# Contiguous token layout, merged sample blocks, and an f32 attention-value product in two column groups

## The reference, cut to what matters

```python
m = silu(c) @ w_ada + b_ada                    # shift, scale and gate, twice
h = layer_norm(x) * (1 + scale1) + shift1
u, q, k, v = split(h @ w_in)                   # 512 columns each
pool = multiscale_pool(u) @ w_pool * pool_scale
z = q @ k.T * 64 ** -0.5                       # strictly causal
a = sigmoid(z)[t, s] * prod_{s < j < t} (1 - sigmoid(z)[t, j])
x = LN1(alpha * x + gate1 * (concat(pool, a @ v) @ w_o))
h = layer_norm(x) * (1 + scale2) + shift2
x = LN2(alpha * x + gate2 * ((silu(h @ w_g) * (h @ w_u)) @ w_down))
```

## Time and profile before

| | |
|---|---|
| median of 3 runs | 2767.44 us (2766.02 to 2767.84) |
| profiled execution, its own time | 2765.61 us |
| its span, first to last instruction | 2763.4 us |
| mean granted TensorE clock | 0.984 of full |
| PE busy | 2622.0 us (95%) |
| DVE busy | 1624.7 us (59%) |
| ACT busy | 1136.4 us (41%) |
| POOL busy | 645.0 us (23%) |

### The profile page before, as it was taken

One profiled execution on the slowest core, in us unless ns is written; L12 is line 12 of the kernel. 1 busy time (PEld: TensorE's weight loads), 2 busy tenths in 40 slices (PEclk: granted clock), 3 DMA queues, 4 the chain that ended last, 5 costly groups with the idle time before them and its releaser, 6 DMA issues.

```text
span 2763.4 us, 39203 instructions
## 1 busy us (share of the span) xinstructions
PE 2622.0 (95%) x15824; PEld 1430.6 (52%) x15824; DVE 1624.7 (59%) x2084; ACT 1136.4 (41%) x1616; POOL 645.0 (23%) x865
## 2 busy tenths in 40 slices
PE   6899899899898888999999999999999999999998
PEld 3444455344344333454566664456666544999733
DVE  4647654799999999889433233544323344644455
ACT  1522232778887888224322223222222322333331
POOL 1300000466666765223211110001111000111100
PEclk9899999999999999999999999999999999999999
DMA  6225678232323110322222224522322345433462
GB/s 233 94 67 201 234 259 237 74 92 73 81 77 85 24 60 13 129 92 86 71 77 84 62 77 130 198 92 77 100 62 74 106 139 166 119 98 88 127 202 104
DMA packets 262542, 308.25 MB, mean 112 GB/s; under 512 B 27694, under 2 KB 221038, under 8 KB 256603
## 3 DMA queue, kind: packets, MB, share of 16 engines
q1 hardware_dynamic: 243354, 236.54, 27.8%
q10 hardware_dynamic: 19008, 69.21, 7.6%
HBM read 267.32 MB, written 38.40 MB: 111 GB/s over the span
## 4 chain that ended last, share of the span: by engine, by line
PE 73%; DVE 14%; issue 5%; ACT 3%; POOL 1%; DMA 1%; SPq 0%; POOLq 0%; DVEq 0%; ACTq 0%
PE ps L2055 34%; PE ps L2089 18%; PE ps L1767 10%; DVE work L1413 3%; PE ps L2006 3%; DVE work L1429 3%; PE ps L1856 2%; PE ps L1880 2%; PE ps L1858 1%; ACT ps L976 1%; DVE work L1410 1%; DVE work L1582 1%; PE ps L1895 1%; DMA pool_dram<-work 1%; DVE work L1288 1%
## 5 line engine op out<-in xcount | busy, mean ns | idle before, releaser
L2055 PE MATMUL ps<-hidden_t,work 128*128 128x384 f16 (+2 forms) x7392 | 946.2, 290 | 0.6 <-DVE work L1632 0.6
L2055 PEld LDWEIGHTS ps<-hidden_t,work 128*128 128x128 f16 x7392 | 646.9, 98 | 298.7 <-issue 2.4
L2089 PE MATMUL ps<-work 128*128 128x512 f16 (+1 forms) x2244 | 489.3, 379 | 0.0
L1767 PE MATMUL ps<-hidden_t,work 128*128 128x512 f16 (+1 forms) x1920 | 355.7, 343 | 12.4 <-DVE hidden_t L1180 7.7
L2089 PEld LDWEIGHTS ps<-work 128*128 128x128 f16 (+1 forms) x2244 | 215.7, 98 | 272.7 <-issue 18.0
L740 POOL TENSOR_TENSOR work<-work 128x512 f32<-128x512 f32 (+2 forms) x320 | 304.9, 955 | 200.4 <-DVE work L1413 128.7
L787 POOL TENSOR_TENSOR work<-work 128x384 f16<-128x384 f32 (+1 forms) x154 | 118.0, 766 | 934.5 <-ACT work L1076 934.5
L1629 DVE SCALAR_TENSOR_TENSOR work<-ps,col,work 128x384 f32<-128x384 f32 (+1 forms) x154 | 80.9, 525 | 431.4 <-ACT work L1074 431.3
L1638 DVE SCALAR_TENSOR_TENSOR work<-work,col 128x1024 f16<-128x1024 f32 x132 | 168.1, 1280 | 227.2 <-ACT work L1086 227.2
L1086 ACT ACTIVATE work<-work,col 128x1024 f16<-128x1024 f32 x132 | 150.8, 1147 | 290.6 <-PE ps L2089 268.9
L1074 ACT ACTIVATE work<-ps,col 128x384 f32<-128x384 f32 (+1 forms) x154 | 77.7, 505 | 450.6 <-PE ps L2055 450.6
(11 more groups left out here) (209 smaller groups left out, 2442.9 us busy)
## 6 DMA issues: line engine op xcount, KB each, us to landing
work<-in_w_gu SPq DMA_DIRECT2D x132, 512.0 KB, 5.0
work<-in_w_down ACTq DMA_DIRECT2D x132, 512.0 KB, 3.6
work<-in_w_ada SPq DMA_DIRECT2D x24, 1024.0 KB, 5.3
work<-in_w_gu SPq DMA_DIRECT2D x22, 1024.0 KB, 5.4
work<-in_w_down SPq DMA_DIRECT2D x11, 1024.0 KB, 5.5
work<-in_x_prompt SPq DMA_DIRECT2D x8, 1024.0 KB, 7.0
work<-in_w_in SPq DMA_DIRECT2D x16, 512.0 KB, 6.7
out<-work SPq DMA_DIRECT2D x32, 256.0 KB, 5.6
```

The costliest lines, as they stand in the source:

```text
L1767: mm = pe.matmul(bank(blk, n, blk), B_HL[s][:, wh * KD * P + k * P:wh * KD * P + (k + 1) * P], moving(k, xh, blk), start=(k == 0 and (wh, ...
L2055: mm = pe.matmul(out, E_GHL[s][:, wh, k, w, :], x, start=(k == 0 and (wh, xh) == (0, 0)), stop=(k == KD - 1 and (wh, xh) == TERMS[-1]))
L2089: mm = pe.matmul(ps[0:rows, 2 * slot + half, :], E_HID[:, j, xh, at:at + rows], E_DHL[slab_home(g)][:, wh, 512 * half:512 * (half + 1)], s ...
```

## The change

What it does:

- `hidden_t` becomes [partition, k, part, 2080 tokens], the sample's 32 tokens right behind the prompt's 2048. `project` takes five blocks of 416 columns instead of 4 x 512 + 32, and the last gate/up group two blocks of 272 instead of 256, 256 and 32. `token_rows` waits for the block in which its 512 tokens end. `evac_pool` copies the last 32 columns of its last block separately.
- The attention weights stay f32: one copy of each turned tile, by ACT for three of four tiles and by DVE for every fourth (k % 4 == 1), scaled by `C_SMIX`. `weigh` multiplies them by the raw f32 values (64 columns), even key tiles into rows 0 to 63 of the bank and odd ones into rows 64 to 127, and PE's loop issues two `weigh` together every second step. On the diagonal a product with zeros opens rows 64 to 127. The value splits go. SP loads the next values after the queries and keys, once all weighing of the head before is done.
- Products with few stationary columns are spread over the four groups of 32 columns: the `w_ada` products at the start and in the attention, the mixing output of the sample, and the down products of the sample tile. The four parts are added by a product with `fold` (four stacked identities, [128, 32]); for the conditioning rows by an f32 product with `SEL`, its first two columns, in place of the transpose. Before `fold` is applied ACT (mixing) or DVE (down) copies 128 x 1024 out of PSUM.
- The sample tile moves behind tile 12 in the order of `down`'s fifth pass.

The diff, cut to its core:

```diff
-        hidden_t = sb("hidden_t", [P, NT + 1, KD, 2, P], f16)
+        cond_t = sb("cond_t", [P, KD, TS], f32)
+        fold = sb("fold", [P, TS], f32)
+        hidden_t = sb("hidden_t", [P, KD, 2, TOK], f16)
...
+        PB = TOK // 5
+        def copied(k):
+            by_dve = (k + 3) // 4
+            return (at_dve, by_dve) if k % 4 == 1 else (at_act, k + 1 - by_dve)
...
-        E_BLKS = [((0, 3), (3, 3)), ((6, 3), (9, 3)), ((12, 2), (14, 2), (NT, 1))]
+        E_BLKS = [((0, 384), (384, 384)), ((768, 384), (1152, 384)), ((1536, 272), (1808, 272))]
-        LN2_TILES = [*range(12), NT, *range(12, NT)]
+        LN2_TILES = [*range(13), NT, *range(13, NT)]
-                  ((9, 1), (10, 2), (11, 3)), ((12, 3), (13, 0)), ((14, 1), (15, 2), (16, 3))]
+                  ((9, 1), (10, 2), (11, 3)), ((12, 2), (13, 3)), ((14, 0), (15, 1), (16, 2))]
...
-                    sp.wait_ge(v_lo, h)
-                    load_v((h + 1) // 2, (h + 1) % 2)
                     sp.wait_ge(z_mm, 4 * NU * h)
                     load_qk((h + 1) // 2, (h + 1) % 2)
+                    sp.wait_ge(av_mm, 4 * NU * h)
+                    load_v((h + 1) // 2, (h + 1) % 2)
...
-            def at_high(k):
+            def at_copy(k):
                 act.wait_ge(at_mm, k + 1)
                 if k >= 4:
                     act.wait_ge(av_mm, k - 3)
-                act.activation(C_AT[k % 4][:, 0, j0:BLK], ps[:, 4 + k % 2, j0:BLK], ACT.Identity,
-                               scale=2.0 ** TOP).then_inc(at_act, 1)
+                act.activation(C_AT[k % 4][:, j0:BLK], ps[:, 4 + k % 2, j0:BLK], ACT.Identity,
+                               scale=c1(C_SMIX)).then_inc(at_act, 1)
...
-                if 5 <= m < NTILE + 5:
-                    at_high(m - 5)
+                if 5 <= m < NTILE + 5 and m % 4 != 2:
+                    at_copy(m - 5)
...
             for t in range(15):
+                if t == 14:
+                    act.wait_ge(so_mm, 2)
+                    act.activation(E_TMP, ps[:, 6:8, :].rearrange("p a n -> p (a n)"), ACT.Identity).then_inc(parts_copied, 1)
...
-            def at_low(k):
-                v.wait_ge(at_act, k + 1)
-                v.scalar_tensor_tensor(C_AT[k % 4][:, 1, j0:BLK], ps[:, 4 + k % 2, j0:BLK], 2.0 ** TOP,
-                                       C_AT[k % 4][:, 0, j0:BLK], ALU.mult, ALU.subtract).then_inc(at_dve, 1)
+            def at_copy(k):
+                v.wait_ge(at_mm, k + 1)
+                v.tensor_scalar(C_AT[k % 4][:, j0:BLK], ps[:, 4 + k % 2, j0:BLK], c1(C_SMIX), None,
+                                ALU.mult).then_inc(at_dve, 1)
...
-                    mm = pe.matmul(ps[0:2, s % 2, 0:256], CT[:, :, k], A_WADA[:, s, k, :],
-                                   start=(k == 0), stop=(k == KD - 1))
+                    at = TS * (k % 4)
+                    mm = pe.matmul(ps[at:at + TS, 2 + s % 2, 256:512], CT[:, k, :], A_WADA[:, s, k, :],
+                                   start=(k < 4), stop=(k >= 4))
...
             def weigh(k):
-                pe.wait_ge(at_dve, k + 1)
-                pe.matmul(ps[:, 6 + b % 2, j0:BLK], C_VHL[:, e, 4 * kc + kt, :], C_AT[k % 4][:, 0, j0:BLK],
-                          start=(kc == b and kt == 0), stop=(kc == 0 and kt == 3), skip_group_check=True)
-                pe.matmul(ps[0:HD, 6 + b % 2, j0:BLK], C_VHL[:, e, 4 * kc + kt, 0:HD], C_AT[k % 4][:, 1, j0:BLK],
-                          start=False, stop=(kc == 0 and kt == 3), skip_group_check=True).then_inc(av_mm, 1)
+                e, r = h % 2, HD * (kt % 2)
+                pe.wait_ge(*copied(k))
+                if kc == b and kt == 1:
+                    pe.matmul(ps[HD:P, 6 + b % 2, 0:P], C_TRI[:, 0:HD], ident_b[:, :], start=True, stop=False,
+                              skip_group_check=True)
+                pe.matmul(ps[r:r + HD, 6 + b % 2, j0:BLK], C_V[e][:, 4 * kc + kt, :], C_AT[k % 4][:, j0:BLK],
+                          start=(kc == b and kt < 2), stop=(kc == 0 and kt >= 2),
+                          skip_group_check=True).then_inc(av_mm, 1)
...
-                if m >= 7:
+                if m >= 8 and m % 2 == 0:
+                    weigh(m - 8)
                     weigh(m - 7)
...
+            def mix_out_sample():
+                for n in range(2):
+                    for i in range(3 * KD):
+                        k, (xh, wh) = i // 3, TERMS[i % 3]
+                        at = TS * (i % 4)
+                        mm = pe.matmul(ps[at:at + TS, 6 + n, :], hidden_t[:, k, xh, SEQ:TOK],
+                                       D_WO[k][:, wh, 512 * n:512 * (n + 1)], start=(i < 4), stop=(i >= 3 * KD - 4))
+            def fold_sample(bank0, done):
+                for n in range(2):
+                    mm = pe.matmul(ps[0:TS, bank0 + n, :], fold[:, :], E_TMP[:, 512 * n:512 * (n + 1)],
+                                   start=True, stop=True)
...
+                            if tile == NT:
+                                r, ends = TS * ((m + half) % 4), 4
+                    if p == 5 and (j, i) == (1, 2):
+                        pe.wait_ge(parts_copied, 2)
+                        fold_sample(6, parts_sum)
```

More of the change, by code:

```diff
@@ L284, in leave, with tile_cols @@
                 self.reg = None
[L286 to L295, removed]
+        PB = TOK // 5
+        def tile_cols(t):
+            return slice(t * P, t * P + P) if t < NT else slice(SEQ, TOK)
         TERMS = [(0, 0), (0, 1), (1, 0)]
@@ L747, in head_split @@
                 r = slice(HD * (h % 2), HD * (h % 2) + HD)
-                st = C_ST[b % 2][r, :].rearrange("p (i t) -> p i t", t=P)
-                dst = [hidden_t[r, 4 * b:4 * b + 4, 4 + h // 2, half, :] for half in range(2)]
+                st = C_ST[b % 2][r, :]
+                dst = [hidden_t[r, 4 + h // 2, half, BLK * b:BLK * (b + 1)] for half in range(2)]
                 pool.wait_ge(o_scaled, blk + 1)
@@ L905, in _ @@
                     act.wait_ge(q_stored[u], 32)
-                evac(c, u, B_QT[u])
+                for blk in range(5):
+                    evac(c, u, B_QT[u], blk)
                 high_part(c, B_QT[u])
             wpool_evac(3)
-            def evac_rows(c, s, blk):
-                act.wait_ge(proj_mm, 5 * c + blk + 1)
-                at, n = (BLK * blk, BLK) if blk < 4 else (SEQ, TS)
-                act.activation(B_VT[s][:, at:at + n], ps[:, blk, 0:n], ACT.Identity,
-                               scale=c1(C_W + 2 * s + 1)).then_inc(proj_out, 1)
             def rows_out(m):
@@ L1695, in _ @@
                         for n in first:
-                            summed(n)
+                            if LN2_TILES[n] == NT:
+                                parts_out(n)
+                            else:
+                                summed(n)
                     if 3 <= j < 3 + 2 * len(first):
                         (counted, normed)[(j - 3) % 2](first[(j - 3) // 2])
+                    if grp == 2 and j == 4:
+                        summed(first[1])
                 if grp < 2:
@@ L1739, in _ @@
             for q in range(16):
-                mm = pe.transpose(ps[:, 2, 2 * q:2 * q + 2], A_MROW[0:2, q * P:(q + 1) * P], ident[0:2, 0:2])
+                mm = pe.matmul(ps[:, 2, 2 * q:2 * q + 2], A_MROW[:, q * P:(q + 1) * P], SEL, start=True, stop=True)
             mm.then_inc(mod_turned, 1)
@@ L2087, in down @@
                     for half in range(2):
-                        for wh, xh in TERMS:
-                            mm = pe.matmul(ps[0:rows, 2 * slot + half, :], E_HID[:, j, xh, at:at + rows],
+                        for term, (wh, xh) in enumerate(TERMS):
+                            m = 3 * j + term
+                            if tile == NT:
+                                r, ends = TS * ((m + half) % 4), 4
+                            else:
+                                r, ends = 0, 1
+                            mm = pe.matmul(ps[r:r + rows, 2 * slot + half, :], E_HID[:, j, xh, at:at + rows],
                                            E_DHL[slab_home(g)][:, wh, 512 * half:512 * (half + 1)],
-                                           start=(j == 0 and (wh, xh) == (0, 0)),
-                                           stop=(j == NF - 1 and (wh, xh) == TERMS[-1]))
+                                           start=(m < ends), stop=(m >= 3 * NF - ends))
                     mm.then_inc(dn_mm, 1)
+                    if p == 5 and (j, i) == (1, 2):
+                        pe.wait_ge(parts_copied, 2)
+                        fold_sample(6, parts_sum)
             for grp in range(3):
```

228 lines of the change are left out of this document (108 added, 120 removed).

## The result

The changed kernel takes 2652.4 us, median of 4 runs (2648.2 to 2656.6), against 2766.7 us (2765.4 to 2767.8) for the kernel before on the same chip: a ratio of 0.9587, interval 0.957 to 0.9604. The profiled execution has a span of 2654.9 us, 108.5 under the span before.

| stage | before, us | after, us | difference | forecast |
|---|---|---|---|---|
| start, to the first projection | 77.6 | 74.0 | -3.6 | +4 |
| projections, to the first weighing | 431.3 | 430.2 | -1.1 | -3.5 |
| attention | 597.1 | 508.7 | -88.4 | -52 |
| mixing output | 205.2 | 208.5 | +3.3 | 0 |
| gate/up and down | 1452.2 | 1433.5 | -18.7 | -24 |

A forecast was written before the change was run, and what follows sets the result against it. VectorE was taken to bound the attention, and PE's streaming rate everything from 1311 us on. The sum was 2765.6 - 52 - 13 - 3.5 - 11 + 4 = 2690 us, 2692 on the median, range 2662 to 2762.

The forecast's parts named there:

- if B1 streams beside A2: Attention weighing: odd tile's first f32 instruction overlaps even tile's second, 1.52 us a pair (1.96 serial); 52 us gained.
- the pieces: Attention's 16 conditioning pieces, f32 products with w_ada: from 3.6 us each to nine slots, 2.0 us, plus 0.3 for turning.
- The pace: Attention time per head: PE's load of 60.8 us plus 12% for waits gives 68 us, from 74.6.
- Neither bounds any longer: Attention: with DVE down to about 414 us and ACT to about 437, neither sets the time.
- Latency: Attention rival: groups overlap, but the chain scan, scores, two sigmoids, scan sets 72 us a head; 2725 us, chance 0.10.
- absorbed case: Attention rival: no group overlap, PE's loss shrinks to 5%, 74.9 us a head, attention unchanged; 2757 us, chance 0.11.
- slower rival: Attention rival: no group overlap, f32 pair 1.96 us or more, 12% loss stays, 79.9 us a head; 2799 us, chance 0.12.
- The rule on weight loads: Attention, counter-argument: loads overlap products only across row groups, so a pair grows by four loads; given little weight.
- Gate/up: Last gate/up group: 32-column instructions go, 29.8 us, and 272-column ones cost 13.8 more; 13 us gained, 10 to 16.
- Down: Sample's down products: column groups cut PE to 2.0 us a slab, late slabs hold it at 2.2; 11 us gained.
- Mixing output: Sample's mixing output: groups save some 8 us of PE but gain 0, because DVE's chain sets the stage.
- Start: Start: w_ada products run at 0.98 of the DMA engines, so only the last piece gains, 1.5 us; stage forecast +4.

The follow-up runs named there:

- one_group: Changed kernel with both tiles of a pair weighed in the lower columns, f32 weights kept: 2699.5 us, ratio 0.9752 to the kernel before.
- sig_together: Changed kernel with the two sigmoid instructions of a pair of tiles issued one behind the other: 2658.3 us, ratio 0.9603 to the kernel before.
- ada_att_old: Changed kernel with only the attention's 16 conditioning pieces back on two stationary columns: 2683.5 us, ratio 0.969 to the kernel before.
- down_old: Changed kernel with the sample's down products back in one column group, without copy and fold: 2656.4 us, ratio 0.9593 to the kernel before.
- raw_ring: Changed kernel with five raw w_down slab buffers instead of three in the fifth pass, loads issued four slabs ahead instead of two: 2640.2 us, ratio 0.9545.
- mix_old: Changed kernel with the sample's mixing output back in one column group, without the fold: 2651.6 us, ratio 0.958 to the kernel before.
- f16_weights: Changed kernel with only the attention's weighing back to f16 high and low parts and split values: 2722.9 us, ratio 0.9829 to the kernel before.
- ada_start_old: Changed kernel with the start's w_ada products and their turning back on two columns, four bf16 products added: 2660.8 us, ratio 0.9606.

## Why the prediction was right and wrong

- **Attention, wrong in size (88 for 52).** The step that failed is "if B1 streams beside A2": it counted one overlap in four instructions, and there are two. The term of the sum that rests on it is the attention's 52 us. A pair's weighing takes 1.1 us with the changes of width, not 1.52, and PE's part of a pair 2.85 us, not 3.27. The same fault sits in the pieces: nine slots and 2.0 us forecast, four and 1.0 measured. The Trainium skill, TensorEngine Tiling (Array Packing), Key Properties, says that tiles run loads and products in parallel; one_group and the trace of after bear it out, and its rule fits 1.1 better than the 1.52 for which I cited it: I had kept A1 ahead of B1 without a reason from a row or from that page.
- **The pace.** With the right prices PE's 60.8 us a head becomes 60.8 - 12 x 0.42 - 4 x 0.5 - 2 x 1.0 = 52 (57 by the profile's busy time, which counts the tails of runs too). The pace is 508.7/8 = 63.6, 9% above ACT's 58.6. "Neither bounds any longer" holds at 68 us a head and not here. ACT was forecast at 437 us and has 468; 20 of the 31 are the copies, 148.2 us for 240, where three quarters of the earlier trace rows would be 128.
- **The rivals.** Latency had 72 us a head, and 63.6 were measured, with sig_together gaining nothing. The overlap sets both others aside, and one_group bears on their prices: serial f32 weighing alone gives 2699.5 us. With the pieces undone too (31 us by ada_att_old; the two were not run together) it would be about 2730, an estimate, under the 2757 of the absorbed case. The slower rival is far off. Three sums are off by little: the latency case adds up to 2723, not 2725, the low end of the range by its own terms to 2665, not 2662, and PE's serial load to 71.5 us a head, not 71.3.
- **The rule on weight loads.** The trace of after decides: the loads for A1, B1, A2, B2 start 0, 6, 55 and 61 ns after the first, all on the same rows, and the last two run while A1 streams. The Trainium skill, TensorE: Matmul & The Clock Gate, Part 3, which has a load overlap a product only with another row group, does not hold here. Nor is it the column group that makes the difference: in one_group, with all four in the same rows and columns, the second load starts 55 ns after the first, while A1 streams, and the third 2 ns after A2 has started.
- **Gate/up, right:** 13 forecast, 12.4 measured. **Projections:** 3.5 forecast, 1.1 measured. The rate is right (23.18 us for each of the chunks 9 to 14 before, 22.96 after, so 3.5 us for 16), but the first chunk takes 43.7 us for 40.5, where the start's sum allowed for 1.
- **Down, half right.** The mechanism (slabs late at 2.2 us) is what the runs show. 11 us were forecast and about 4 came: from the first product of the fifth pass to the end of the sixth it is 147.1 us before, 142.9 after and 147.3 in down_old. The fifth gains 11.0 us of the 13 forecast (61.5 to 50.5; 2.3 us a slab, not 2.2), and the sixth loses 6.8 again: 1.9 for the fold, as forecast; 3.5 in its first slab, where PE waits 2.9 us for DVE to take a sum out of the bank that it needs (DVE came late from the slabs' splits); and 1.2 in the second, where the clock is at its 1.2 GHz level for 3.4 us after that wait. The last two were missing in the sum; in raw_ring the sixth loses only the 2 us of the fold.
- **Luck, 1.7 us.** The rest of the 18.7 us of this stage is 0.4 us that the mixing output had lost and, in the first group's gate/up, a stretch of 3.4 us at 1.2 GHz that before had and the changed kernel has not. From the first product behind the mixing output's last turn to the first down product it is 331.0 us in every trace with such a stretch, and 329.3 in every one without it.
- **Mixing output.** The 0 for the column groups is right (mix_old); yet the stage grew by 3.3 us. 2.9 of them lie between the first products of tiles 7 and 9, and they are the clock's, beside the sample's value products. In all 14 traces that stretch takes 30.7 us when the clock is at its 1.2 GHz level for 3.4 us of it (before, f16_weights, one_group), 32.0 to 32.1 for 6.8 us, and 33.5 to 33.7 for 10.2 us (the changed kernel and others). f16_weights and one_group have the changed kernel's mixing code, so it is not the code of this stage. Why the level holds longer in some is open. The last 0.4 us come back in the first gate/up step.
- **Start, wrong in sign (-3.6 for +4).** The failed step is "the w_ada products run at 0.98 of the DMA engines, so only the last piece gains". The mean over 15 to 45 us hid that w_ada was loaded at 33.8 us, with PE 11.4 us behind: PE was the bound, and the groups let it keep up with loads that run as before. The turning's price, taken as +2.4 or double, was +3.3, and the slower turns of tokens before it, 0.9 at the lower clock, were not counted.

Still open: what sets the distance of 9% between ACT's load and the pace of a head, and why the clock's low stretches differ in length.

## What to carry to other kernels

In this kernel products in disjoint column groups of PE run side by side, f32 ones too: when a kernel has narrow products (64 or 32 columns), put them into groups and count slots as the largest number of instructions in any one group, not as their sum. In that form an f32 product costs PE less than the high/low split did (1.1 us a pair for 2 x 0.64), and takes the split's vector work away. After such a gain, take the stage's busy times again: ACT went from 82% of the attention to 92%, and the w_down loads came to set the fifth pass, where two more buffers, and loads issued four slabs ahead, gave the next 12 us. And before a load is called the bound, compare when its last piece lands with when the work on it ends: a mean over the stretch hid 11 us here.

## What the hardware showed that was not expected

- Both passes of an f32 product keep the pairing: A1 and B1 start 7 ns apart, A2 and B2 too, 480 ns later.
- Products do not start in program order when their groups differ. The six f16 down products of a slab go to groups a, a+1, a+2, a+1, a+2, a+3. The first three start at 2520.287, .291 and .294 us, the last at .304, before the fourth and fifth, at .518 and .521, whose groups are taken until then. The last one carries the semaphore's increment, and the increment does not come early: in all 22 slabs it comes 26 to 29 ns after the end, as the trace models it, of the latest of the six, and 230 to 234 ns after that of the instruction which carries it.
- A product of 32 columns of tokens costs about a quarter in four groups: 48 of 512 columns take 2.77 us in the mixing output, 58 ns each, and 10.5 us in one group.
- PE loses clock where it has gaps: 0.74 of full in 15 to 37.3 us and 0.59 to 74 us in the changed kernel, against 1.00 and 0.68 in the earlier trace rows; in ada_start_old, where PE has no gaps in that stretch, it is 1.00 again.
